# A 31-tap depthwise convolution moved onto full-height TensorE matmuls, with a DRAM bounce for shifted copies, merged waits and 512-wide value projections

## What is computed

```
glu = a * sigmoid(b)                                  # 256 x 512
y[t, ch] = sum_{j=0..30} glu[t - 30 + j, ch] * w_dw[j, ch] + b_dw[ch]   # depthwise, causal
out = silu(layernorm(y) * ln_g + ln_b)
```

## Time and profile before

| what | us |
|---|---|
| median of 3 runs (1566.84 to 1567.78) | 1567.77 |
| the profiled execution's own time | 1568.06 |
| its span, first to last instruction | 1566.3 |
| PE busy (99% of the span) | 1546.9 |
| DVE busy (71%) | 1111.9 |
| ACT busy (53%) | 836.1 |
| POOL busy (5%) | 78.9 |

### The profile page before, as it was taken

How to read it: one execution, slowest core, us unless ns; L and a number is a source line. 1 busy time by engine, 2 the same in 40 slices (tenths; PEclk the granted TensorE clock), 3 DMA queues, 4 the chain that set the end, 5 groups by cost and what they waited for, 6 DMA issues and landing times.

```text
span 1566.3 us, 25162 instructions
## 1 busy us (share of the span) xinstructions
PE 1546.9 (99%) x9726; PEld 1353.9 (86%) x9726; DVE 1111.9 (71%) x1574; ACT 836.1 (53%) x1170; POOL 78.9 (5%) x173
## 2 busy tenths in 40 slices
PE   8999999999999999999999999999999999999997
PEld 7888899998888888889989888888888997888886
DVE  6776668668666776665756866678766787876666
ACT  6564556555445555455555644555544643554544
POOL 0400002000000000000000081000000000000000
PEclk9999999999999999999999999999999999999999
DMA  9865554545655564655434565456555451655551
GB/s 302 239 214 190 181 169 135 189 135 190 213 187 172 169 219 166 213 187 162 162 118 152 189 213 188 168 176 223 180 208 178 125 180 55 206 198 193 186 192 50
DMA packets 208534, 280.72 MB, mean 179 GB/s; under 512 B 5182, under 2 KB 183784, under 8 KB 208456
## 3 DMA queue, kind: packets, MB, share of 16 engines
q1 hardware_dynamic: 206080, 274.50, 52.6%
q0 software_dynamic: 1360, 3.80, 0.9%
q10 hardware_dynamic: 1016, 1.32, 0.3%
HBM read 278.55 MB, written 2.63 MB: 180 GB/s over the span
## 4 chain that ended last, share of the span: by engine, by line
PE 90%; DVE 5%; ACT 2%; DMA 2%; issue 1%; SPq 0%; DVEq 0%; ACTq 0%
PE bank L1614 42%; PE bank L1665 28%; PE bank L1664 12%; DVE w_lo L977 2%; PE bank L1667 2%; PE bank L1723 1%; DMA raw<-in_ffn_w_gate 1%; PE bank L2103 1%; PE bank L1877 1%; ACT w_hi L533 1%; PE bank L1848 1%; DMA raw<-in_ffn_w_up 1%; PE bank L1866 1%; ACT xT L561 0%; DVE arena L1128 0%
## 5 line engine op out<-in xcount | busy, mean ns | idle before, releaser
L977 DVE TENSOR_TENSOR w_lo<-raw,w_hi 128x1024 fp32r<-128x1024 f32 x514 | 614.6, 1224 | 216.8 <-ACT w_hi L533 215.9
L1665 PE MATMUL bank<-xT,w_hi 128*128 128x512 f32 x2112 | 733.5, 396 | 3.4 <-DVE memT_lo L1017 1.4
L533 ACT ACTIVATE w_hi<-raw 128x1024 fp32r<-128x1024 f32 x514 | 528.0, 1052 | 148.8 <-PE bank L1665 82.7
L1664 PE MATMUL bank<-xT,w_lo 128*128 128x256 f32 x1848 | 515.7, 279 | 0.8 <-DVE xT L1017 0.8
L1665 PEld LDWEIGHTS bank<-xT,w_hi 128*128 128x128 f32 x2112 | 382.4, 188 | 77.7 <-DVE memT_lo L1017 1.6
L1664 PEld LDWEIGHTS bank<-xT,w_lo 128*128 128x128 f32 x1848 | 348.3, 188 | 13.0 <-DVE w_lo L1246 1.1
L1614 PE MATMUL bank<-w_hi,hid_hi 128*128 128x512 f32 x528 | 207.1, 392 | 0.2 <-DVE hid_lo L1133 0.2
L1614 PE MATMUL bank<-w_hi,hid_lo 128*128 128x512 f32 x528 | 205.6, 389 | 0.0
L1614 PE MATMUL bank<-w_lo,hid_hi 128*128 128x512 f32 x528 | 205.5, 389 | 0.0
L1614 PE MATMUL bank<-xT,w_hi 128*128 128x256 f32 x800 | 145.9, 285 | 0.3 <-DVE w_lo L977 0.3
L1614 PEld LDWEIGHTS bank<-xT,w_hi 128*128 128x128 f32 x800 | 125.2, 192 | 1.5 <-DVE w_lo L977 0.5
(11 more groups left out here) (263 smaller groups left out, 1600.2 us busy)
## 6 DMA issues: line engine op xcount, KB each, us to landing
raw<-in_ffn_w_down SPq DMA_DIRECT2D x44, 1024.0 KB, 5.5
raw<-in_ffn_w_in SPq DMA_DIRECT2D x44, 1024.0 KB, 5.2
raw<-in_ffn_w_gate SPq DMA_DIRECT2D x43, 1024.0 KB, 5.4
raw<-in_ffn_w_up SPq DMA_DIRECT2D x43, 1024.0 KB, 5.4
raw<-in_ffn_w_out SPq DMA_DIRECT2D x22, 1024.0 KB, 5.4
raw<-in_w_in SPq DMA_DIRECT2D x10, 1024.0 KB, 5.4
raw<-in_xa_w_kv SPq DMA_DIRECT2D x8, 1024.0 KB, 5.2
raw<-in_od_w_in SPq DMA_DIRECT2D x8, 1024.0 KB, 5.5
```

Of the source, the lines that this page charges most:

```text
L533: act.activation(hi, src, ACT.Copy).then_inc(sem["hi_ready"], 1)
L977: dve.tensor_tensor(lo, src, hi.bitcast(F32), ALU.subtract).then_inc(sem["lo_ready"], 1)
L1664: pe.matmul(bank[:, b, T:2 * T], lo, xT_hi[:, k, :], start=False, stop=False)
L1665: last = pe.matmul(bank[:, b, :], hi, xT[:, k, :, :], start=k == 0, stop=k == KD - 1)
```

## The change

Four things, besides moves that follow from them. (1) All four convolution tiles run on PE with 128 rows of contraction: four groups of 8 taps (the 32nd has weight zero) are stacked along the partitions, for 32 channels at a time. The shifted copies (`strips`) are made by storing `glu` to DRAM and loading it four times at offsets of 8 columns; ACT issues two stores and eight loads. (2) The four value projections use 512 output columns per matmul (`wide_rows`). (3) Waits are merged or moved: step 0 of the first FFN, the memory transposes in two parts after `down` of steps 5 and 6, the root of the last norm behind the splits. (4) The root of the first 128 rows at the end is finished on POOL, and their scaling comes later on ACT.

```diff
+    def wide_units(w, c0):
+        for k in (0, 4):
+            units.append((WIDE, w.rearrange("(k p) f -> p k f", p=P)[:, k:k + 4, c0:c0 + 512]))
...
+        strips = [arena[:, at:at + groups_of_pair * STRIP].rearrange("p (g c) -> p g c", c=STRIP) for at in (7268, 2120)]
...
-                for tile in range(1 - half, 2):
-                    with pool.Fori(0, CONV_TAPS) as j:
+                for tile in range(2):
+                    with pool.Fori(0, CONV_STEPS) as j:
+                        for n in range(CONV_STRIPS):
...
+            pool.wait_ge(sem["first_guess"], 1)
+            step(pool.tensor_tensor(u, y, y, ALU.mult))
...
+            step(pool.tensor_tensor(final_rstd[:, 0:1], w, y, ALU.mult))
...
+                if f.v0 == 0 and j == 0:
+                    gate_low()
                 for n in range(2):
                     split(i, base + n)
-                gate_low()
+                if f.v0 or j:
+                    gate_low()
...
+            def glu_store(pair):
+                act.wait_ge(sem["glu_ready"], pair + 1)
+                act.dma_start(rows[:, 2 * pair:2 * pair + 2, :], glu[:, 2 * pair:2 * pair + 2, :])\
+                    .then_inc(sem["glu_stored"], 16)
+            def strip_loads(pair, name):
+                act.wait_ge(sem["glu_stored"], 16 * (pair + 1))
+                for r in range(CONV_STRIPS):
+                    shifted = bass.AP(glu_dram.tensor, pair * 2 * P * GLU_WIDTH + r * CONV_STEPS,
+                                      [[GLU_WIDTH, CONV_GROUP], [CONV_GROUP * GLU_WIDTH, groups_of_pair], [1, STRIP]])
+                    act.dma_start(strips[pair][r * CONV_GROUP:(r + 1) * CONV_GROUP, :, :], shifted)\
+                        .then_inc(sem[name], 16)
...
-            evac_nat(v + 16, g_v[:, :, 0:T], 1)
-            splits(2)
+            act.wait_ge(sem["gla_scores"], 2)
+            strip_loads(0, "first_strips_loaded")
+            glu_store(1)
             c.next("k_nat_psum")
             act.activation(k_nat, bank[:, 4, :], ACT.Copy).then_inc(sem["k_nat_ready"], 1)
-            evac_nat(v + 18, g_v[:, :, T:2 * T], 2)
-            splits(2)
+            splits(2)
+            strip_loads(1, "second_strips_loaded")
+            splits(2)
+            evac_rows(v + 18, g_v, 1)
...
             gate(1, 0, 512)
-            act.wait_ge(sem["final_rstd_ready"], 1)
-            act.activation(result[:, 0, :], result[:, 0, :], ACT.Copy, scale=final_rstd[:, 0:1])
+            square(1, 0, 512, 2)
             act.wait_ge(sem["half_done"], n_half)
             gate(1, 512, 768)
             gate(1, 768, D)
-            square(1, 0, 512, 2)
             square(1, 512, 768, 3)
             square(1, 768, D, 4)
+            act.wait_ge(sem["pool_root"], POOL_ROOT_STEPS)
+            act.activation(result[:, 0, :], result[:, 0, :], ACT.Copy, scale=final_rstd[:, 0:1])
...
+            link(dve.memset(glu[:, :, PAD + T:GLU_WIDTH], 0.0))
...
+            glu_product(0)
             scaled(v + 14, sig_b[:, 2:4, :], 5)
             splits(2)
+            glu_product(1)
...
-            norm(COL_OF["ple_2"], scale=0.5, n_done=end)
+            norm(COL_OF["ple_2"], scale=0.5, n_done=end, with_root=False)
             splits(10)
+            rstd_of_both("ple_rstd_ready")
...
+            def wide_rows(b, xs):
+                for n in range(4):
+                    v = take()
+                    split_ready(v, None)
+                    for t in range(NT):
+                        for i in range(2):
+                            k = 2 * n + i
+                            last = products(bank[:, b + t, :], tuple(m[:, k, t * P:(t + 1) * P] for m in xs),
+                                            w_cols(v, i, 512), k == 0, k == KD - 1)
+                        if n == 3 and t == 0:
+                            last.then_inc(sem["first_rows"], 1)
+                    last.then_inc(sem["half_done"], 1)
...
-                        if j == 5 and i is None and n in (0, 2):
+                        if j in (6, 7) and i is None and n == 2:
                             c.next("xT_lo_ready", 2)
...
+                for j in range(CONV_STEPS):
+                    for n in range(CONV_STRIPS):
+                        last = pe.matmul(bank[n * CONV_GROUP:(n + 1) * CONV_GROUP, CONV_BANK[tile], 0:T],
+                                         weights[:, j * CONV_STRIPS + n, :],
+                                         strips[tile // 2][:, tile % 2 * CONV_STRIPS + n, j:j + T],
+                                         start=j == 0, stop=j == CONV_STEPS - 1)
```

More of the change, by code:

```diff
@@ L45 @@
 MASKED = -1e38
-ROWS, COLS, PAIRED, RANK = "rows", "cols", "paired", "rank"
+ROWS, COLS, PAIRED, RANK, WIDE = "rows", "cols", "paired", "rank", "wide"
 GATE_RANK = 16
@@ L671, in evac_nat, with evac_rows @@
                 last.then_inc(sem["nat_sb"], 1)
+            def evac_rows(n, dst, b, scaled=True):
+                for t in range(NT):
+                    if t == 0:
+                        c.next("first_rows")
+                    else:
+                        act.wait_ge(sem["half_done"], n)
+                    act.activation(dst[:, t, :], bank[:, b + t, :], ACT.Copy, scale=rstd[:, t:t + 1] if scaled else 1.0)\
+                        .then_inc(sem["nat_sb"], 1)
             def halves(m):
@@ L797, in cross @@
                     pass
-                for n in range(2):
-                    evac(v + 6 + 2 * n, mem_v[:, :, n * T:(n + 1) * T], 6 + n, src=halves(bank[:, 6 + n, :]))
-                    if n == 0:
-                        splits(2)
+                splits(2)
+                evac_rows(v + 8, mem_v, 6, scaled=False)
                 probT_copies(XA_GROUPS, 0)
@@ L819, in _ @@
             soft = softmax_exp(MOBA_GROUPS, False)
[L820 to L823, removed]
-                splits(2)
+            for _ in range(3):
+                next(soft)
+            splits(2)
+            for _ in range(3):
+                next(soft)
+            evac_rows(v + 16, v_sb, 6)
+            splits(2)
             evac(v + 18, mem_k[:, 0:2, :], 6, src=halves(bank[:, 6, :]))
@@ L1434, in _, with glu_product @@
             splits(4)
-            scaled(v + 14, sig_b[:, 2:4, :], 5)
-            splits(2)
-            for n in range(2):
+            def glu_product(n):
                 dve.wait_ge(sem["nat_sb"], NAT_BEFORE_2 + 2 + 2 * n)
@@ L1442, in _ @@
                      "glu_ready")
-            def conv_parts():
-                c.next("conv_psum")
-                dve.tensor_copy(conv_part[:, 2:4, :], bank[:, CONV_BANKS[2]:CONV_BANKS[3] + 1, 0:T])\
-                    .then_inc(sem["conv_part_ready"], 1)
+            glu_product(0)
+            scaled(v + 14, sig_b[:, 2:4, :], 5)
+            splits(2)
+            glu_product(1)
             c.next("gla_scores", 2)
@@ L1902, in memory @@
                         at = (k % 2) * T + t * P
[L1903 removed]
+                        last = pe.transpose(bank[:, 2 + k % 4 // 2, at:at + P], mem_in[:, t, k * P:(k + 1) * P], ident[:, :])
                     if k % 2:
@@ L2007, in _ @@
                              lambda h, nk: k_sb[:, h // 2, 0:nk], which)
-            for b in (6, 7):
-                nat_unit(b, X)
+            wide_rows(6, X)
             for b in (6, 7):
@@ L2097, in conv_tile @@
                 weights = tap_weights(tile)
[L2098 to L2116 removed]
+                for j in range(CONV_STEPS):
[4 more added lines that the diff above has]
+                                         start=j == 0, stop=j == CONV_STEPS - 1)
+                last.then_inc(sem["conv_psum"], 1)
+            pe.wait_ge(sem["tap_diags"], 4 * CONV_STEPS * CONV_STRIPS)
             c.next("score_ready", 4)
```

246 lines of the change are left out of this document (126 added, 120 removed), and 2 rows, old and new, of the table AX.

## The result

The changed kernel took 1557.71 us (median of 4 runs, 1557.38 to 1559.59) beside 1567.72 us of the kernel before, measured in the same session: 0.9942 of it, 95% interval 0.9928 to 0.9956. It is faster by 10.0 us. 12.1 were forecast, with 1555.7 us for the median; the time lies within the range of 1553.5 to 1561, but 2.0 above the forecast, which is more than the 1.5 that its main chance allowed. The profiled execution took 1557.92 us with a span of 1556.2; PE is busy for 1541.2 us (1546.9 before), DVE for 1096.2, ACT for 833.2, POOL for 93.2.

What follows compares the result with a forecast made beforehand. TensorE, busy 99% of the span, was taken as the bound. Gains 6.3 + 2.4 + 1.0 + 1.4 + 0.6 + 0.7 less 0.2 and 0.1 gave 12.1 us: 1556.0 profiled, 1555.7 median; range 1553.5 to 1561.

Steps and rivals of the forecast that it cites:

- step 0 of the first FFN: Start of first FFN: DVE's sum placed ahead of a split lets PE restart at 21.2 instead of 23.03; gain 1.0 us.
- memory transposes: First FFN: four channel groups are copied while PE does two halves of `gate_up`, removing PE's wait; gain 1.4 us.
- four wide units: Two cross attentions, MoBA, GLA v: 96 matmuls at 0.120 become 48 at 0.227; 0.6 each, 2.4 us in all.
- convolution: Convolution stage: four tiles of 16 rounds at 0.227 us take 14.5 instead of 20.8; gain 6.3 us.
- last norm: Last norm: small operations move behind the five splits, so PE's wait for the last split goes; gain 0.6 us.
- end: After PE's last matmul: ACT's last gates start about 1557.3, DVE takes its half at 1557.9 instead of 1558.63; gain 0.7 us.
- Rival A: New convolution tiles: weight loads show, four tiles take 22.8 us instead of 14.5; 1564.0 us; chance 0.08.
- PE needs the next of these halves more than 5 us later: Second mixer: work queued behind ACT's two new waits, k's copy and four splits, reaches PE in time; cost 0.
- rival B: One new wait: late GLA gate, bank not free, or ACT held by DMA waits; 2 to 5 us, 1558 to 1561; chance 0.19.
- rival C: End of kernel: POOL's root is late, all after it 1.9 us later than the sum; 1557.6 us; chance 0.06.
- E: DRAM bounce late by more than its 4 us cover, or promise otherwise unkept: same time as before or above; chance 0.04.
- D: Convolution strips run one after another: 58 us for four tiles, 1599 us, slower than before; chance 0.03.

Runs made afterwards that it cites:

- the kernel with the values still later: Changed kernel with the two evictions of GLA's v on ACT put behind four wide splits instead of two: 1562.3 us, 0.9962 of the kernel before.
- the in-turn kernel: Changed kernel with conv_tile's two loops exchanged, so all eight steps of one strip run before the next strip: 1590.57 us in one run.
- the kernel with the table early: Changed kernel plus one 128 x 1 sigmoid on ACT behind the last splits, loading the activation table early: 1558.72 us, 0.9943 of the kernel before.

## Why the prediction was right, and where it was off

| step | forecast, us | measured, us |
|---|---|---|
| step 0 of the first FFN, memory transposes, one more transpose | 1.0 + 1.4 - 0.1 = 2.3 | 1.8 + 1.7 - 0.35 - 0.3 (before it starts) = 2.8 (trace); step 0 alone 1.16 (undone) |
| four wide units | 2.4 | 0.56 + 0.55 + 0.56 + 0.6 = 2.3 |
| memset | -0.2 | -0.13 (trace) |
| convolution | 6.3 | 6.5 for the tiles, 0.26 for the mean |
| what stands behind ACT's new waits | 0 | -2.1, and the fallen clock |
| last norm | 0.6 | 0.78 (trace), 0.85 (undone) |
| end | 0.7 | 0.0 |

**The convolution.** A round was taken at 0.227 us and measured 0.226. That it would be near the fold's 0.28 or below, and not the old tiles' 0.356, rested on the fold and the 64-column strips, which were of the new shape: shape decided better than length. The exact value was partly luck. It was borrowed from 512 columns in one fast pass, without a reason why 256 float32 columns should take the same; the row of these instructions one after another was read as 0.249 each, but held 0.26 us more than the same eight take in the mean and the variance of the changed kernel, 1.73 us or 0.216 each. Rival A (weight loads visible, 1564.0) is refuted: a round of four with a new weight load for each instruction takes 0.226, hardly more than that. The weight loads (PEld) of a tile lie within 3.20 us, beside the 3.68 of its matmuls:

```profile
1302.27 3.20 PEld L2178 LDWEIGHTS bank<-arena,memT_lo 128*32 128x32 f32 x64
1302.27 3.68 PE L2178 MATMUL bank<-arena,memT_lo 128*32 128x256 f32 x64
```

The rule that the Trainium skill states in TensorE: Matmul & The Clock Gate, Part 3: Packing small matmuls, that a weight load overlaps matmuls in flight only when it goes to another group of rows, does not describe these strips: every load and every matmul here uses all 128 rows, and they still run together. Why the old tiles took 0.356 a round stays open.

**The step that failed: "PE needs the next of these halves more than 5 us later".** The prediction asked what stands behind ACT's new waits and named the copy of k and four splits. It left out the eviction of GLA's v, which is queued behind the same wait and which PE needs at once for the chunk states. It had reckoned with 9.5 us for a transfer of that size, but with no landing time for the second store, whose 8.19 us fix when ACT comes free: it had the second pair's loads issued about 6 us behind the first pair's, and they were issued 10.2 us behind (1276.05 and 1265.90). This is rival B by kind (ACT held by its DMA waits), though the place was not seen, and it cost 2.1 us by the trace and 2.4 to 2.5 by the medians of the two kernels without it. The cause is shown twice: by moving what was waiting, and by making the store land earlier. The prediction had said that it would be wrong if a new wait of PE over 2 us appeared in the second mixer, and this wait is 2.1: so the range was met, and this part of the mechanism was not. The time is also where rival C had put it, 1557.6, but by chance, since C's cause did not occur.

**The end.** The term of 0.7 came out as nothing, and 0.75 to 0.81 us came back with the table loaded early. The prediction had taken ACT's gates for ready at PE's end. The first gate was 1.28 us late by the table load, which in the new code stands behind the wait for PE's sums; everything on ACT and DVE there is a chain, so that the delay was carried to the last gates. In the old code one wait stood ahead of that gate, in the new code two. That the compiler puts the load between them is what the traces suggest; no run took one of the two waits away. POOL's root was in time (rival C did not come: 3.75 us for ten steps, 0.375 each, where up to 0.57 were allowed), and taking it from DVE is worth 1.2 us once the table is out of the way. The 0.7 was therefore there to be had, and was spent on the table. A small slip of the prediction, 1557.3 for the last gates where its 1556.8 + 0.3 is 1557.1, changes nothing in this.

**The transfers.** The first pair's last load landed at 1275.38, 13.3 us after the scores' end (forecast 13.5) and ahead of the first tile at 1282.71. PE never waited for strips, and the cost of the bounce through DRAM itself was 0, as forecast (E did not come). It was not free for the weights, though: the 1 MB loads issued from 1255 to 1290 us landed after 8.0 us at the median, where it was 5.0 before. The changed kernel had room for that; the kernel with the values still later had not. D was excluded by the fold, rightly; the in-turn kernel shows that it would have come with the loops exchanged.

**What stays open.** Why the granted clock falls behind this wait in some executions and not in others: it fell with waits of 2.2, 2.3 and 5.9 us, and did not with 2.1 and with 3.0. And the 2.7 us outside the span in one execution of the kernel with the table early. The memory transposes and the four wide units were not put back one at a time; their 1.7 and 2.3 us are read from the shifts of the trace alone.

## What to carry to other kernels

When a wait is put into an engine's queue, list every instruction behind it up to the point where it would have been free, and find for each the first engine that needs it; one forgotten eviction cost more here than any of the moved waits brought. Price a new matmul pattern by the row of the same shape and order, however short, and keep neighbours in program order on different column strips. An effect under 1 us is measured on a kernel whose larger, varying wait has been taken away first.

## What the runs showed of the hardware that was not expected

- A store of 288 KB landed in 4.0 to 4.6 us with no strip loads ahead of it on ACT's queue, and in 8.1 to 8.8 us with four loads of 263 KB ahead of it.
- In the kernel before, the three weight loads of 1 MB issued from 1268 to 1284 us landed in 4.8 to 5.0 us; in the changed kernel, those issued at 1271 and 1280 us, with strip loads on the way, took 11.1 and 9.5.
- Behind a wait of PE of 2.3 us the granted clock was 1.2 GHz for 3.4 us in one profile; behind 2.1 us it was 2.4 GHz throughout in another. The falls cost 1.6 and 2.3 us.
- Four strips of 32 columns with 128 rows and 256 float32 columns moving: 0.056 us an instruction in rotation, 0.179 in turn.
- POOL's operations on 128 x 1 values took 0.19 us in six of ten cases, and 0.23 to 0.66 in the other four, three of them TENSOR_SCALAR.
